# Attention biases loaded in the layer before, a compressed attention branch staged further apart, and more identity products in a two-block transformer kernel

## The chip, the cores and the metric

The kernel runs on one core of a Trainium2 chip. A core has TensorE (PE in the profile, its weight loads PEld), VectorE (DVE), ScalarE (ACT), GpSimd (POOL) and SyncE (SP). Each takes its own instructions in order and waits on semaphores for the others. Data moves from HBM in DMA transfers, which here are issued by ACT and by SP, each on a queue of its own; the profile writes ACTq and SPq for the issuing. The metric is the device time of one execution in microseconds (us). Everything is float32.

## What is computed

Two blocks in a row on 256 tokens of width 1024. The first block has two layers: a sparse attention with three branches (compressed, selected, window; with 256 tokens all four blocks are selected) and a block attention that is plain causal attention at this length. The second block has one layer: eight heads of windowed attention with a table bias and eight heads of 2-D neighbourhood attention with a relative bias, then a retrieval of single-neuron experts (16 384 of them, all evaluated here). The parts that the change touches, cut from the reference:

```
# layer 0, compressed branch
k_cmp = partial_rope(rms_norm(compress(kc, 0), k_g[0]), cos_c, sin_c)
v_cmp = compress(vc, 1)
p_cmp = masked_softmax(einsum('bcgrd,bngd->bcgrn', qc, k_cmp) * scale, m_cmp)
o_cmp = einsum('bcgrn,bngd->bcgrd', p_cmp, v_cmp)
return gc[..., 0:1] * o_cmp + gc[..., 1:2] * o_slc + gc[..., 2:3] * o_win
# every layer
h = rms_norm(x, norm_g[i]) * (1 + scale) + shift        # scale, shift, gate from c @ ada_w
x = x + gate * ((o * silu(z)) @ w_out)
# second block: scores + bias, then softmax; both mixers normalised before w_out
mixed = concatenate([rms_norm(o_a, out_norm_a), rms_norm(o_b, out_norm_b)])
x = x + gate1 * (mixed @ w_out)
```

## The kernel before

Tokens lie in two tiles t of 128. The program is straight-line up to the experts, and one emission order in Python sets the order of instructions on each engine. The stages: layer 0 (sparse attention) to about 245 us of the span, layer 1 to about 375, layer 2 (windowed and neighbourhood attention) to about 515, then the query products and the experts.

**Projections.** A weight tile of 2 MB (`Tile`) is loaded by ACT's queue into one of three ring slots; `load_all` issues the loads of the tiles named in a call. Most tiles are split into a high and a low part (`Parts.step`: ACT copies a quarter to `u_hi` or `v_hi`, DVE forms `u_lo` or `v_lo`), and PE makes three products of them (`project_split`, `project_cols_split`, line 688, 24 products a block of columns). A quarter of the next tile is split while PE works on a block of this one.

**Deferred work.** `soon(work, delay, summed)` puts a piece of work on a list with a due time on `pe_us`, a running estimate of PE's time; `run_later()` emits what is due after each block of products. Work marked `summed` is left out of the `run_later(True, False)` that comes ahead of an attention. In layer 0 the transposes of the queries (L864, copy L866 on ACT) and six stages of the compressed branch are placed so: `run_turns(0)`, `cmp_scores(0)` (L1433: 16 products; its softmax from L1440 to L1463 on DVE with one exponential on ACT), `run_turns(1)`, `cmp_turned(0)` (L1468, copy L1471), `cmp_scores(1)`, `cmp_turned(1)`. They lie among the eight blocks of the z projection, z0 and z1, whose results go through ACT (L1174).

**Adaptive-norm weights.** 80 chunks of 512 KB (`in_ada_t`) come on SP's queue into three buffers; `trickle` emits one DVE step for each (L429), spread over all projections and attentions. When one is used, its buffer's next chunk is asked for.

**Attention.** `attend` walks pairs p of banks: exponentials of p (L965 on DVE, L973 on ACT), the normalising of p-1 (L1001 or L1005), scores of p+1 (L954), outputs of p-2 (L923), transposes of p-1 (L1014, copies L1017 on ACT). At p == 3 it issues the loads of its `loads` argument. `fill_wait(n, b)` (L188) makes n products of the identity with itself into a bank that nobody reads; at p == 1 it is called with fills[0] and fills[1].

**Output stages.** `gated_out.rest` multiplies the attention's result with w_out; near its end, at (t, c) == (1, 5), `turn_next` transposes the next layer's normalised tile 0 (L568), which waits for ACT's scaling (L605). In layer 2 `normed` squares the result (L1627) and `sum_squares` sums it by products with ones (L1640).

**Biases of layer 2.** `bias_a` (1.5 MB) is loaded after the first query products of layer 2, `bias_b` (2 MB) after the second, both on ACT's queue (L156), between the loads of the tiles kb, vb_tile, mix_out0 and mix_out1.

Of the kernel before, what the change touches and what calls it, by code (L numbers as in the profile page):

```python
# [48 lines left out]
LAYER_ROOM = 18027  # L49
TOK = 4  # L50
# [75 lines left out]
def build(nc, st, a, dbg):  # L126
# [28 lines left out]
    def load(dst, src, name, eng=None):  # L155
        return Load(nc, st, name).did((eng or sy).dma_start(dst, src))  # L156
# [47 lines left out]
    def soon(work, delay=0.0, summed=False):  # L204

        item = Pending(work, pe_us[0] + delay, summed)
        later.append(item)
        return item
# [641 lines left out]
    def q_tile_use(qT, j, tab_g, bufs):  # L850

        def use(t, ps, m):
# [4 lines left out]
            def second():  # L857
# [12 lines left out]
                turns[t] = soon(turn_over, TURN_LAG)  # L870
# [218 lines left out]
    def gated_out(first, second, layer, tmp, rstd=None):  # L1089
# [41 lines left out]
        def rest(begin_next, turn_next, place_next, loads):  # L1131
# [8 lines left out]
            for t in range(NT):  # L1140
                x_hi, x_lo = (h[:, :, t * P:(t + 1) * P] for h in (h_hi, h_lo))
                for n, cs in enumerate(halves):
                    b = proj_bank()
                    T.need(b.free, h_split[t])
                    for c in cs:
                        if (t, c) == (NT - 1, DC - 3):
                            turn_next()
                            place_next()
# [67 lines left out]
    with ExitStack() as s0:  # L1216
# [198 lines left out]
        project_split(q1, q_tile_use(qT, 1, row("nsa_q_norm"), qbufs), z0, (z1,))  # L1415
# [70 lines left out]
        def run_stage(n):  # L1486
            f, t = stages[n]
            f(t)
            if n + 1 < len(stages):
                soon(lambda: run_stage(n + 1), (2.5, 3.5, 3.5, 0.5, 7.5)[n])  # L1490

        soon(lambda: run_stage(0), 1.0)
# [30 lines left out]

    with ExitStack() as s1:
# [6 lines left out]
        zT = carve([P, DC, S], s1)  # L1531
        split_h(0, V)
# [13 lines left out]
               causal_bias, lambda h: 3e38, True, [copied["q"], copied["k"]], [copied["v"]], lambda t: None, times_z(zT), tail, (qa,), (1, 3, 1))  # L1546
# [10 lines left out]
    with ExitStack() as s2:  # L1557
        w_in = a["w_in_2"]
        bias_a = carve([P, HA, 3 * P], s2)
        bias_b = carve([P, NT, HB, S], s2)  # L1560
# [15 lines left out]
        m_ba = load(bias_a[:], a["bias_a"], "ld_ba", ac)  # L1576
# [19 lines left out]
        m_bb = load(bias_b[:], a["bias_b"], "ld_bb", ac)  # L1596
# [16 lines left out]
        def bias_of(h, t, w):  # L1613
            return bias_a[:, h, P * (1 - t):P * (3 - t)] if h < HA else bias_b[:, t, h - HA, :]
# [7 lines left out]
        def normed(t, m):  # L1622
# [12 lines left out]
            def sum_squares():  # L1635
                b = spare_bank()
                T.need(b.free, m_s, m_ones)
# [13 lines left out]
        tail, rest = gated_out(mix_out0, mix_out1, 2, [carve([P, 512], s2) for _ in range(NT)], lambda t, half: rstds[:, t, half:half + 1])  # L1651
# [4 lines left out]
               bias_of, lambda h: nsink[:, h:h + 1] if h < HA else 3e38, False, [*m_ready, m_ba, m_bb], [m_vb], lambda t: None,  # L1656
               normed, tail, (query0,), (2, 4, 1), sink=row("sink_a_2"))
# [599 lines left out]
```

## Time and profile before

| | us |
|---|---|
| three runs | 1368.34, 1369.69, 1370.37; median 1369.69 |
| the profiled execution | 1369.69, of it span of the instructions 1368.4 |
| PE busy in the span | 1293.2 (95%) |
| DVE, ACT, POOL busy | 1064.2 (78%), 596.6 (44%), 245.7 (18%) |
| mean granted TensorE clock | 0.985 of full speed |

A row of a timeline gives start and duration in us, engine, line, operation, the tensors and shapes and how many are merged; in brackets stands how long the engine had been idle and who released it. Matmul rows count two for each product in float32. `ACTq` rows are DMA issues: their duration is that of the issuing, not of the transfer. Line numbers are those of the kernel before.

### The profile page before, as it was taken

To read this page: it belongs to the slowest core of one execution; us is meant where nothing else is said; L and a number is where in the kernel's file an instruction comes from. 1 tells how busy PE (TensorE), PEld (TensorE's weight loads), DVE (VectorE), ACT (ScalarE), POOL (GpSimd) and SP (SyncE) were. 2 spreads that over 40 slices of the span, in tenths; PEclk is the share of its full clock that TensorE was granted. 3 is DMA by queue.
4 is the path that set the end of the run, shared out by engine and by line. 5 is a ranking of instruction groups with operands and counts; after the bars stand their busy time and mean duration, and the time that the engine had idled before them with its cause. 6 is when DMAs were issued, how large, how long until landed. Compare 5 with 4: busy or idle time off the path is not lost.

```text
span 1368.4 us, 21907 instructions
## 1 busy us (share of the span) xinstructions
PE 1293.2 (95%) x8261; PEld 1115.5 (82%) x8261; DVE 1064.2 (78%) x2316; ACT 596.6 (44%) x1101; POOL 245.7 (18%) x179
## 2 busy tenths in 40 slices
PE   5888998988998889999999999999999999999997
PEld 5577865685696569999999999999988888888886
DVE  5686796687667788999997888888876667766676
ACT  1534483546343525455544444444343333333332
POOL 0463000360000005689950000000000000000000
PEclk9998899999999989999999999999999999999999
DMA  9867532866379335454444444444465555555552
GB/s 353 307 223 285 190 124 63 290 214 234 128 285 355 108 130 210 156 183 164 173 139 154 141 153 143 151 147 148 154 214 186 185 188 192 189 185 187 189 192 95
DMA packets 92238, 256.82 MB, mean 188 GB/s; under 512 B 9456, under 2 KB 16880, under 8 KB 91760
## 3 DMA queue, kind: packets, MB, share of 16 engines
q1 hardware_dynamic: 59728, 195.91, 41.6%
q10 hardware_dynamic: 32416, 59.66, 12.3%
q8 instruction: 60, 0.98, 0.3%
q14 instruction: 34, 0.28, 0.1%
HBM read 254.47 MB, written 1.06 MB: 187 GB/s over the span
## 4 chain that ended last, share of the span: by engine, by line
PE 61%; DVE 15%; POOL 9%; issue 7%; DMA 5%; ACT 3%; SPq 1%; POOLq 0%; ACTq 0%; DVEq 0%
PE bank L1714 26%; PE bank L1706 19%; PE bank L1986 4%; PE bank L688 3%; PE bank L1118 3%; POOL v_lo L1746 2%; POOL u_lo L1746 2%; DMA arena<-in_w_in 2%; DVE arena L429 2%; DVE arena L965 2%; POOL head_ms L819 2%; DMA arena<-in_nsa_w_in 1%; DVE u_lo L680 1%; PE bank L714 1%; DVE arena L1005 1%
## 5 line engine op out<-in xcount | busy, mean ns | idle before, releaser
L1706 PE MATMUL bank<-h_hi,u_hi 128*128 128x256 f32 x632 | 182.9, 289 | 3.9 <-POOL u_lo L1746 2.9
L1706 PE MATMUL bank<-h_hi,u_lo 128*128 128x256 f32 x632 | 178.9, 283 | 0.0
L1706 PE MATMUL bank<-h_lo,u_hi 128*128 128x256 f32 x632 | 178.8, 283 | 0.0
L1706 PEld LDWEIGHTS bank<-h_hi,u_hi 128*128 128x128 f32 x632 | 121.1, 192 | 4.8 <-POOL u_lo L1746 1.9
L1706 PEld LDWEIGHTS bank<-h_lo,u_hi 128*128 128x128 f32 x632 | 121.2, 192 | 0.0
L1706 PEld LDWEIGHTS bank<-h_hi,u_lo 128*128 128x128 f32 x632 | 121.0, 191 | 0.0
L2169 POOL TENSOR_SCALAR stat<-stat 128x1 f32<-128x1 f32 x2 | 0.4, 190 | 656.8 <-ACT arena L2166 656.8
L2082 ACT ACTIVATE u_hi<-raw 128x1024 fp32r<-128x1024 f32 x64 | 68.1, 1063 | 108.6 <-PE bank L1714 108.6
L2082 ACT ACTIVATE v_hi<-raw 128x1024 fp32r<-128x1024 f32 x64 | 68.0, 1063 | 106.5 <-PE bank L1714 106.5
L1706 PE MATMUL bank<-h_hi,v_hi 128*128 128x256 f32 x392 | 113.0, 288 | 0.9 <-POOL v_lo L1746 0.9
L429 DVE CUSTOM_DVE_ANT_0 arena<-arena 128x1024 f32<-128x1024 f32 x80 | 102.5, 1293 | 11.9 <-DMA arena<-in_ada_t 10.8
L1706 PE MATMUL bank<-h_hi,v_lo 128*128 128x256 f32 x392 | 111.0, 283 | 0.0
L1706 PE MATMUL bank<-h_lo,v_hi 128*128 128x256 f32 x392 | 110.9, 283 | 0.0
L2088 DVE TENSOR_TENSOR v_lo<-raw,v_hi 128x1024 fp32r<-128x1024 f32 x64 | 78.5, 1226 | 25.4 <-ACT v_hi L2082 25.4
L2088 DVE TENSOR_TENSOR u_lo<-raw,u_hi 128x1024 fp32r<-128x1024 f32 x64 | 78.5, 1226 | 25.3 <-ACT u_hi L2082 25.3
L2016 ACT ACTIVATE gate_row<-bank 128x256 f32<-128x256 f32 (+40 forms) x83 | 23.5, 283 | 167.4 <-PE bank L1706 167.4
L1714 PE MATMUL bank<-u_hi,a_hi 128*128 128x512 f32 x256 | 80.7, 396 | 0.6 <-DVE a_lo L1732 0.6
L1714 PE MATMUL bank<-v_lo,a_hi 128*128 128x512 f32 x256 | 80.8, 397 | 0.0
L1714 PE MATMUL bank<-u_lo,a_hi 128*128 128x512 f32 x256 | 80.7, 397 | 0.0
L1714 PE MATMUL bank<-v_hi,a_hi 128*128 128x512 f32 x256 | 80.6, 396 | 0.0
L1714 PE MATMUL bank<-u_hi,a_lo 128*128 128x512 f32 x256 | 80.0, 393 | 0.0
L1714 PE MATMUL bank<-v_hi,a_lo 128*128 128x512 f32 x256 | 80.0, 393 | 0.0
(273 smaller groups left out, 3480.7 us busy)
## 6 DMA issues: line engine op xcount, KB each, us to landing
raw<-in_u SPq DMA_DIRECT2D x128, 512.0 KB, 3.5
raw<-in_v SPq DMA_DIRECT2D x128, 512.0 KB, 4.3
arena<-in_ada_t SPq DMA_DIRECT2D x80, 512.0 KB, 5.5
arena<-in_ada_w SPq DMA_DIRECT2D x12, 512.0 KB, 12.2
raw<-in_nsa_w_in ACTq DMA_DIRECT2D x3, 2048.0 KB, 11.8
arena<-in_moba_w_in ACTq DMA_DIRECT2D x3, 2048.0 KB, 14.4
arena<-in_w_in ACTq DMA_DIRECT2D x3, 2048.0 KB, 10.5
arena<-in_w_query ACTq DMA_DIRECT2D x3, 2048.0 KB, 10.4
```

The costliest lines, as they stand in the source:

```text
L429: m = V.did(ve.tensor_tensor_reduce(out=chunk_buf[i], in0=chunk_buf[i], in1=silu_row, scale=1.0, scalar=0.0, op0=ALU.mult, op1=ALU.add, ac ...
L688: inst = pe.matmul(dst, x, y, start=first and n == 0, stop=last and n == len(pairs) - 1)
L819: return G.did(po.tensor_tensor(hn[0:np_, 0:n], hn[0:np_, 0:n], pow_half[0:np_, 0:n], ALU.pow))
L965: m = V.did(ve.tensor_tensor_reduce(out=probs[k][:, j * w:(j + 1) * w], in0=b.t[:, j * w:(j + 1) * w], in1=bias_of(h, t, w), scale=-1.0, s ...
L1118: last = pe.matmul(b.t[:], hT[:, c, t * P:(t + 1) * P], first.w[:, c, :], start=c == halves[n][0], stop=c == halves[n][-1])
L1706: last = pe.matmul(zbank[k].t[:, 0:S], u[:, c, :], h[:, c, :], start=n == 0, stop=n == 3 * DC - 1)
L1714: last = pe.matmul(outb[2 * t + h].t[:], x[k][:, t * P:(t + 1) * P], quad[slot][y][:, h * 512:(h + 1) * 512], start=b == 0 and n == 0, sto ...
L1746: po.tensor_tensor(quad[slot][1], raw_all[:, slot, :], quad[slot][0].bitcast(F32), ALU.subtract).then_inc(s_ulo, 1)
L1986: last = pe.matmul(gate_bank(g).t[:, j * P:(j + 1) * P], one_hot[:, g % 2, j, :].bitcast(F32), weighted[:, g % 2, j, :], start=True, stop= ...
L2016: last = ac.activation(zpast[k][:, 0:done], zbank[k].t[:, 0:done], ACT.Gelu_apprx_tanh)
L2082: ac.activation(quad[slot][0], raw_all[:, slot, :], ACT.Copy).then_inc(s_vhi, 1)
L2088: ve.tensor_tensor(quad[slot][1], raw_all[:, slot, :], quad[slot][0].bitcast(F32), ALU.subtract).then_inc(s_vlo, 1)
```

## The change

Three things are done. The biases of layer 2 get a fixed place in the arena's last 6400 columns and, for two heads, in `hkT`, and are loaded as three transfers at p == 3 of layer 1's attention, behind the tile qa; the two loads in layer 2 go. In layer 0 the transposes of the second half of the queries are due 30 instead of 10.5 after their block, the six stages get other delays, and the last one may move into the attention. Identity products are added: two at the end of the output stages of layers 0 and 1, four in that of layer 2, one more at p == 1 of layer 2's attention, and one ahead of each of its two sums of squares.

```diff
@@ constants
 LAYER_ROOM = 18027
+BIAS_AT = ARENA - 6400
@@ q_tile_use: the transposes of a block of queries wait for their time
-    def q_tile_use(qT, j, tab_g, bufs):
+    def q_tile_use(qT, j, tab_g, bufs, lag=TURN_LAG):
...
-                turns[t] = soon(turn_over, TURN_LAG)
+                turns[t] = soon(turn_over, lag)
@@ gated_out, rest()
                         if (t, c) == (NT - 1, DC - 3):
+                            fill_wait((2, 2, 4)[layer], banks[4])
                             turn_next()
                             place_next()
@@ layer 0, the calls
-        project_split(q1, q_tile_use(qT, 1, row("nsa_q_norm"), qbufs), z0, (z1,))
+        project_split(q1, q_tile_use(qT, 1, row("nsa_q_norm"), qbufs, 30.0), z0, (z1,))
@@ layer 0, the stages of the compressed branch
             if n + 1 < len(stages):
-                soon(lambda: run_stage(n + 1), (2.5, 3.5, 3.5, 0.5, 7.5)[n])
-
-        soon(lambda: run_stage(0), 1.0)
+                soon(lambda: run_stage(n + 1), (2.5, 2.5, 2.5, 2.5, 14.0)[n], n + 2 == len(stages))
+
+        soon(lambda: run_stage(0), 2.5)
@@ between layer 0 and layer 1
+    bias_a_most = arena[:, BIAS_AT:BIAS_AT + 6 * 3 * P].rearrange("p (h k) -> p h k", h=6)
+    bias_a_rest = hkT[:].rearrange("p i n -> p (i n)").rearrange("p (h k) -> p h k", h=HA - 6)
+    bias_b = arena[:, BIAS_AT + 6 * 3 * P:ARENA].rearrange("p (t h k) -> p t h k", t=NT, h=HB)
+
+    class Biases:
+
+
+        def load(self, e):
+
+            e.need(halves_done, T.last())
+            self.marks = [load(bias_a_most, a["bias_a"][:, 0:6, :], "ld_ba_most", e.eng),
+                          load(bias_a_rest, a["bias_a"][:, 6:HA, :], "ld_ba_rest", e.eng),
+                          load(bias_b, a["bias_b"], "ld_bb", e.eng)]
+
+    biases, halves_done = Biases(), T.last()
@@ layer 1, the loads of its attend
-               causal_bias, lambda h: 3e38, True, [copied["q"], copied["k"]], [copied["v"]], lambda t: None, times_z(zT), tail, (qa,), (1, 3, 1))
+               causal_bias, lambda h: 3e38, True, [copied["q"], copied["k"]], [copied["v"]], lambda t: None, times_z(zT), tail, (qa, biases), (1, 3, 1))
@@ layer 2
-        bias_a = carve([P, HA, 3 * P], s2)
-        bias_b = carve([P, NT, HB, S], s2)
...
         project_cols_by_tile(qa, q_use(0), qb, (kb,), 4)
-        m_ba = load(bias_a[:], a["bias_a"], "ld_ba", ac)
...
         project_cols_split(qb, q_use(HA // 2), kb, (vb_tile, mix_out0))
-        m_bb = load(bias_b[:], a["bias_b"], "ld_bb", ac)
...
         def bias_of(h, t, w):
-            return bias_a[:, h, P * (1 - t):P * (3 - t)] if h < HA else bias_b[:, t, h - HA, :]
+            if h >= HA:
+                return bias_b[:, t, h - HA, :]
+            return (bias_a_most[:, h] if h < 6 else bias_a_rest[:, h - 6])[:, P * (1 - t):P * (3 - t)]
...
             def sum_squares():
                 b = spare_bank()
+                fill_wait(1, b)
                 T.need(b.free, m_s, m_ones)
...
-               bias_of, lambda h: nsink[:, h:h + 1] if h < HA else 3e38, False, [*m_ready, m_ba, m_bb], [m_vb], lambda t: None,
-               normed, tail, (query0,), (2, 4, 1), sink=row("sink_a_2"))
+               bias_of, lambda h: nsink[:, h:h + 1] if h < HA else 3e38, False, [*m_ready, *biases.marks], [m_vb], lambda t: None,
+               normed, tail, (query0,), (2, 5, 1), sink=row("sink_a_2"))
```

PE in layer 0, from the products of the second compression on. `bank<-hkT` are the folds of the hidden layer (L1327) and of the gates (L1392), `128x32 x16` a `cmp_scores`, `ident,arena 128x128 x4` a set of four transposes (L864 queries, L1468 `cmp_turned`); each "..." stands for blocks of 24 products of L688. Before:

```order
L1302 MATMUL bank<-arena 64x256 x24
L864 MATMUL bank<-ident,arena 128x128 x4
L1327 MATMUL bank<-hkT 128x64 x2
...
L1392 MATMUL bank<-hkT 128x48 x2
...
L864 MATMUL bank<-ident,arena 128x128 x4
L1433 MATMUL bank<-arena 128x32 x16
...
L1468 MATMUL bank<-ident,arena 128x128 x4
L954 MATMUL bank<-arena 128x128 x16
```

The same place now (the lines of after.py are one or two further down):

```order
L1304 MATMUL bank<-arena 64x256 x24
L1329 MATMUL bank<-hkT 128x64 x2
...
L1394 MATMUL bank<-hkT 128x48 x2
L865 MATMUL bank<-ident,arena 128x128 x4
...
L1435 MATMUL bank<-arena 128x32 x16
...
L955 MATMUL bank<-arena 128x128 x16
...
L1470 MATMUL bank<-ident,arena 128x128 x4
L924 MATMUL bank<-arena 64x256 x12
```

The first query transposes now come after the gates' fold, one block of z products stands between them and the scores, the second ones a block later still, and the last transposes of the compressed branch have left the place ahead of the attention's scores for one ahead of its first outputs. On the other side of this, the DVE rows at the end of the z projection, from the second softmax's last step on. `ISA arena,ada` is one adaptive-norm chunk (L429). Before:

```order
L1463 TENSOR_TENSOR arena<-arena 128x512
L429 ISA arena,ada<-arena 128x1024
L429 ISA ada 128x1
...
L436 TENSOR_TENSOR ada<-ada,cols 128x4
L1471 COPY arena<-bank 128x512
L965 ISA arena,nmax<-bank,causal 128x128
```

Now, where "..." stands for two more pairs of the same two rows and, before, for one:

```order
L1465 TENSOR_TENSOR arena<-arena 128x512
L430 ISA arena,ada<-arena 128x1024
L430 ISA ada 128x1
...
L437 TENSOR_TENSOR ada<-ada,cols 128x4
L966 ISA arena,nmax<-bank,causal 128x128
```

Four chunks instead of two stand between the second softmax and the attention, and the copy (L1471) is gone from there. ACT in layer 1's attention, p == 3, now:

```order
L281 DMA arena<-in_w_in 128x8x512
L157 DMA arena<-in_bias_a 128x2304
L157 DMA hkT<-in_bias_a 128x768
L157 DMA arena<-in_bias_b 128x4096
L974 ACTIVATE arena,rsum<-arena,nmax 128x256 x4
```

and ACT in layer 2's projections before, from which the two L156 rows are now gone and nothing else:

```order
L280 DMA arena<-in_w_in 128x8x512
L156 DMA arena<-in_bias_a 128x3072
L677 ACTIVATE u_hi<-arena 128x1024
L1571 ACTIVATE arena<-bank 128x256
L280 DMA arena<-in_w_in 128x8x512
L280 DMA raw<-in_w_out 128x8x512
...
L156 DMA arena<-in_bias_b 128x4096
L677 ACTIVATE u_hi<-arena 128x1024 x2
```

Three issues now stand between one pair's copies and the next pair's exponentials in layer 1; in layer 2 the load of vb_tile (second `in_w_in`) has no bias ahead of it.

## Rows read from the trace of the kernel before

**Rows 1.** The page: shares of the chain that ended last, by engine.

```profile
PE 61%; DVE 15%; POOL 9%; issue 7%; DMA 5%; ACT 3%; SPq 1%; POOLq 0%; ACTq 0%; DVEq 0%
```

**Rows 2.** Windows: us, busy PE PEld DVE ACT POOL, PEclk, DMA share, GB/s.

```profile
134.00:144.00 10.00, 10.00 (x77) 9.94 (x78) 6.03 (x15) 4.52 (x6) 0.00 (x0) 0.70 0.48 184
159.00:172.00 13.00, 11.05 (x76) 9.32 (x78) 11.25 (x61) 9.62 (x37) 0.00 (x0) 0.74 0.67 243
502.00:512.00 10.00, 7.36 (x37) 6.03 (x36) 9.54 (x20) 2.65 (x5) 0.56 (x1) 0.83 0.70 258
```

**Rows 3.** Timeline of PE, layer 0, 121 to 165 us.

```profile
122.61 0.66 PE L1327 MATMUL bank<-hkT 128*128 128x64 f32 x4 [0.68 <-DVE arena L1361]
...
133.85 3.62 PE L1433 MATMUL bank<-arena 64*128 64x32 f32 x32 [3.17 <-ACT arena L866]
...
153.56 1.97 PE L1433 MATMUL bank<-arena 64*128 64x32 f32 x32
...
160.95 1.11 PE L1468 MATMUL bank<-ident,arena 128*128 128x128 f32 x4 [2.34 <-DVE arena L1463]
```

**Rows 4.** Timeline of ACT, layer 0, 130 to 134 us.

```profile
130.31 0.27 ACT L1400 ACTIVATE arena<-arena 128x48 f32<-128x48 f32 x1 [0.28 <-DVE arena L1398]
...
133.12 0.59 ACT L866 ACTIVATE arena<-bank 128x512 f32<-128x512 f32 x1
```

**Rows 5.** Timeline of DVE, end of layer 0's z projection and attention's start.

```profile
155.58 0.76 DVE L1440 TENSOR_TENSOR arena<-bank,cmp_mask 128x256 f32<-128x256 f32 x2 [2.95 <-PE bank L1433]
...
160.20 0.69 DVE L1463 TENSOR_TENSOR arena<-arena 128x512 f32<-128x512 f32 x1
...
163.30 0.68 DVE L1471 COPY arena<-bank 128x512 f32<-128x512 f32 x1
164.12 0.29 DVE L965 CUSTOM_DVE_ANT_0 arena<-bank,causal 128x128 f32<-128x128 f32 x1
```

**Rows 6.** Timeline of DVE, start of layer 1's attention.

```profile
314.90 0.29 DVE L965 CUSTOM_DVE_ANT_0 arena<-bank,causal 128x128 f32<-128x128 f32 x1 [1.87 <-PE bank L954]
```

**Rows 7.** Timeline of PE, layer 2, first and last of four such rows.

```profile
418.85 0.50 PE L688 MATMUL bank<-u_hi,h_hi 128*128 128x512 f32 x1 [1.18 <-DVE arena L1600]
...
426.55 0.50 PE L688 MATMUL bank<-v_hi,h_hi 128*128 128x512 f32 x1 [0.95 <-DVE v_lo L680]
```

**Rows 8.** Timeline of ACT and its queue, layer 2, 395 to 420 us.

```profile
398.22 0.38 ACTq L280 DMA_DIRECT2D arena<-in_w_in  x1
...
406.19 6.24 ACTq L156 DMA_DIRECT2D arena<-in_bias_b  x1
...
416.14 2.01 ACT L677 ACTIVATE u_hi<-arena 128x1024 fp32r<-128x1024 f32 x2 [8.63 <-DMA arena<-in_w_in]
```

**Rows 9.** DMA issues of 385 to 440 us: KB each, median us to landing.

```profile
arena<-in_bias_a ACTq DMA_DIRECT2D x1, 1536.0 KB, 15.5
arena<-in_ada_t SPq DMA_DIRECT2D x15, 512.0 KB, 7.2
```

**Rows 10.** DMA issues of 300 to 330 us.

```profile
arena<-in_ada_t SPq DMA_DIRECT2D x8, 512.0 KB, 4.2
arena<-in_w_in ACTq DMA_DIRECT2D x1, 2048.0 KB, 9.0
```

**Rows 11.** Timeline of ACT, layer 1's attention, behind the load at p == 3.

```profile
331.20 0.51 ACT L973 ACTIVATE arena<-arena,nmax 128x256 f32<-128x256 f32 x1 [1.50 <-DVE nmax L965]
```

**Rows 12.** Timeline of DVE, 387 to 430 us, first and last of four such rows.

```profile
395.94 1.23 DVE L429 CUSTOM_DVE_ANT_0 arena<-arena 128x1024 f32<-128x1024 f32 x1 [1.47 <-DMA arena<-in_ada_t]
...
429.41 1.23 DVE L429 CUSTOM_DVE_ANT_0 arena<-arena 128x1024 f32<-128x1024 f32 x1 [2.58 <-DMA arena<-in_ada_t]
```

**Rows 13.** Timeline of PE, layer 2's attention and output stage.

```profile
438.36 2.00 PE L188 MATMUL bank<-ident 128*128 128x256 f32 x8
...
480.67 2.97 PE L1640 MATMUL bank<-ones,arena 128*128 128x1 f32 x16 [1.18 <-ACT arena L1627]
...
505.46 1.97 PE L568 MATMUL bank<-ident,arena 128*128 128x128 f32 x8 [2.60 <-ACT arena L605]
```

More of the change, by code:

```diff
@@ L1531, in build @@
         zT = carve([P, DC, S], s1)
+        assert top[0] <= BIAS_AT, top[0]
         split_h(0, V)
@@ L1649, in normed @@
             return oz_mark[t]
-        tail, rest = gated_out(mix_out0, mix_out1, 2, [carve([P, 512], s2) for _ in range(NT)], lambda t, half: rstds[:, t, half:half + 1])
+        mix_tmp = [carve([P, 512], s2) for _ in range(NT)]
+        assert top[0] <= BIAS_AT, top[0]
+        tail, rest = gated_out(mix_out0, mix_out1, 2, mix_tmp, lambda t, half: rstds[:, t, half:half + 1])
         attend([(lambda h, w: kaT[half_of(h), h // (HA // KVA), 0:w] if h < HA else kbT[half_of(h), (h - HA) // 2, 0:w],
```

## The prediction

> **What bounds the kernel now.** The table of busy times comes first: PE works 1293.2 of 1368.4 us, so what it does not work is 75 us in all, and an edit can only take from that, from products run at the lower clock, or from DVE where DVE sets the pace. The chain that ended last says the same: 61% on PE, 15% on DVE [rows 1]. So I went through the windows for the granted clock and then through PE's timeline for its waits. The reader is to see three places. In layer 0, among the z products, PE waits 0.68, 3.17 and 2.34 us [rows 3], and the clock is at 0.70 and 0.74 of full speed around the last two [rows 2]. In layer 2, from 417 to 427 us, PE waits four times for the split of vb_tile; the first and the last are in [rows 7], and with 0.82 and 0.96 between them they make 3.91 us. At layer 2's end PE waits 2.60 us for ACT's scaling, and the transposes behind it take 1.97 us [rows 13] in a stretch at clock 0.83 [rows 2]. Behind each place PE or DVE goes on without slack, so I let a gain there pass to the end unless a later wait takes it back.
>
> All sums are against the profiled execution, 1369.69 us, which is also the median of the three runs.
>
> **Layer 0, the z projection.** The first wait (0.68) is the fold's for a bank that DVE's copy L1361 empties late; with the query transposes gone from ahead of it, the fold takes the next bank in turn, which is free, and I expect the wait to go. Before, the copy L866 that lets `cmp_scores(0)` go ran at 133.12 for 0.59 us, though ACT had been free of the gates' sigmoid at 130.31 + 0.27 = 130.58 [rows 4]; other ACT work stood between. Now L866 follows the sigmoid directly, ends near 130.58 + 0.59 = 131.2, and `cmp_scores(0)` can start near 131.3 instead of 133.85: 2.55 us sooner, the 0.68 included. The second query transposes stood ahead of that point and now stand behind it; a set of four took 1.11 us in a slow stretch [rows 3], by the ratio of 3.62 to 1.97 some 0.6 at full clock, which is given back: 1.95 remain. `cmp_turned(0)` needs the first softmax. Its work on DVE and ACT ends 5.3 us after it starts (155.58 to 160.89 for the second one [rows 5]), and DVE will start it late by one split of 1.2 us and a rest, I take 1.9 behind the end of the scores. PE in the meantime has two blocks of products where it had four; a block is some 2.9 us (158.61 less the end of the second scores at 155.53 is 3.1, a pipeline's tail in it) [rows 3]. So PE arrives after 2 x 2.9 + 0.6 = 6.4 and the softmax after 7.2 us: a new wait of 0.8. The waits give 1.95 - 0.8, about 1.2 us.
>
> The clock is the unknown. At 0.70 over 134 to 144 us [rows 2] the products lost 0.30 x 10 = 3.0 us; the scores took 3.62 us there and 1.97 at full speed [rows 3]. If a wait of about 1.95 instead of 3.17 us keeps the clock up, all 3.0 come back; if not, none. The trace has no row that decides between them, so I take the middle, 1.5. The z projection, which ended at 160.95 - 2.34 = 158.61, then ends at T = 155.9: 2.7 us sooner, with bounds of 1.2 and 4.2.
>
> **Layer 0, the entry to the attention.** Before, DVE's first L965 came at 164.12, 5.5 us behind the end of the z products: a wait of 2.34 for the softmax, 1.11 of transposes, the copy of 0.68 and the products of scores. Now three blocks instead of one stand behind the second scores, and the softmax, which ends 5.4 us behind its scores, is through at T - 8.7 + 5.4 = T - 3.3. Four chunk steps of 1.23 us [rows 12] then stand on DVE ahead of L965. Three of them end at T + 0.4. The fourth needs the buffer that the first frees at T - 2.1; a chunk lands in 4.2 us [rows 10], so it runs from T + 2.1 to T + 3.3, and L965 follows. That is 2.2 us better than 5.5. Bounds: in layer 1, where no tail of this kind stands, DVE waited for the scores alone [rows 6], and by the scores alone L965 could come at T + 1.8 (3.7 better); with a landing of 7.2 us [rows 9] it comes at T + 6.3 (0.8 worse). Against this stand the transposes and the copy of the last stage, which are now inside an attention in which DVE sets the pace: 0.68 for the copy [rows 5], up to 1.3 if PE's transposes count too. **Layer 0 in sum: 2.7 + 2.2 - 0.7 = 4.2 us.**
>
> **Layer 1.** Three loads are issued on ACT at p == 3. The first load of a bias needs its columns free, which the program ties to the end of layer 0; that is long past. The issue of vb_tile took 0.38 us and that of a bias behind two big loads 6.24 us [rows 8]. Here only qa is ahead, so I take 0.4 to 0.6 each, 1.8 for the three, near the quick row. What is queued behind them is ACT's exponentials of the next pair, which come after an idle time of 1.50 us [rows 11]. So 0.3 us shows. On the other side, 3 x 6.24 = 18.7 us less 1.50 is the price of issues that block; that is a rival below. The 3.5 MB run beside the ada_t chunks. Eight chunks were asked for in 30 us [rows 10], one in 3.75 us, and three buffers lie ahead, so a chunk has some 11 us to land; 4.2 or even 7.2 [rows 9, 10] is within that. I cost it at nothing; what it costs when the cover is gone is a rival too. The two identity products at the output stages of layers 0 and 1 are 0.5 us each: four took 2.00 [rows 13]. They lie in waits for ACT like the one at 505.46; I cost them at nothing, at most 0.5 each.
>
> **Layer 2, the tile vb_tile.** It was issued at 398.22 and landed at 416.14 [rows 8], 17.9 us later. bias_a, 1.5 MB asked for shortly before on the same queue, itself took 15.5 us [rows 9]. A tile of the same 2 MB with no bias beside it landed in 9.0 [rows 10]. Without the bias I expect 9 to 13 us, thus 407 to 411. What it must beat: the split of the last quarter came 3.9 us too late in all, so a landing 3.9 to 4.4 us earlier, before about 411.7, takes all four waits. Both ends are inside; **3.9 us** go, at worst 2 if the transfers of mix_out0 and the chunks hold it back. DVE's waits for chunks in this stretch (1.47, 1.85, 1.11, 2.58; first and last in [rows 12]) get shorter too, but PE does not wait for them, and I count nothing. ACT no longer issues for 0.6 and 6.24 us; it was idle behind that, for 8.63 us [rows 8].
>
> **Layer 2, attention and output.** One more product at p == 1 fits into PE's wait there: nothing, at most 0.5. The product ahead of each sum of squares: the second lies in a wait of 1.18 us [rows 13], the first where DVE sets the pace. Nothing from the waits. The four ahead of the transposes take 4 x 0.5 = 2.0 us of a wait of 2.60, so they delay nothing. If the clock stays up over them, the stretch of 502 to 512 us gets back 0.17 x 10 = **1.7 us** [rows 2]; if not, 0. I take 1.7, because a quarter of the wait or less is left idle.
>
> **The sum.** -4.2 + 0.3 - 3.9 - 1.7 = -9.5: 1360.2 us.
>
> **Rivals.** (1) The restaging only moves its waits: the clock still falls after 1.95 us, and the buffer of the fourth chunk comes late by the 7.2 us row, so that 1.2, the -0.8 and the -0.7 of the copy leave nothing. For it: the wait moved before too, with each stage hanging on ACT and DVE in turn. Then 1360.2 + 4.2 = 1364.4. (2) vb_tile is still late, since mix_out0 is issued right behind it and shares the transfers: +3.9, 1364.1. Against it: it lands behind everything else in its queue only if later loads overtake it. (3) The clock stays up in more places: the other 1.5 of layer 0, and in the second sum of squares, which took 2.97 us [rows 13]; by the ratio of 3.62 to 1.97 [rows 3] it would take 1.6, 1.4 less. 1360.2 - 2.9 = 1357.3. (4) The chunks of ada_t starve in layer 1's attention. In 387 to 430 us, with a bias and two tiles in flight, DVE waited four times for a chunk, 7.0 us in all [rows 12]. The same mix is now moved to where DVE sets the pace: +7.0, 1367.2. Against it stands the 11 us of lead. (5) The slower one: ACT is held in the three issues at p == 3. If each takes the 6.24 us of [rows 8] instead of 0.6, the exponentials of the next pair, and with them DVE and PE, stand for 18.7 - 1.5 = 17.2 us, and the time is 1360.2 - 0.3 + 17.2 = 1377.1. It ends above the time before once the issues hold ACT for more than 9.8 + 1.5 = 11.3 us in all. For it: three big loads stood behind each other in that row, as they do here with qa and two biases. Against it: there the queue had vb_tile and mix_out0, 4 MB, ahead of it; here the third issue has 3.9 MB less one bias, 3.5 MB, ahead, which have been running for a few us.
>
> The Trainium skill bears on rival 4: "DMA: Bandwidth & Descriptors", section "Queues, rings and completion order", says that each transfer engine takes turns between the queues that have work for it, a packet at a time. By that rule the biases on ACT's queue halve what a chunk on SP's queue gets, whatever order they were asked for in; the landing of 7.2 instead of 4.2 us [rows 9, 10] agrees with it, and it does not by itself exceed the lead.
>
> **How the numbers follow.** Forecast 0.38 (1360.2), rival 1 0.20, rival 2 0.10, rival 3 0.17, rival 4 0.08, rival 5 0.07. A measurement of this kernel can tell about 0.2%, 2.7 us, from no change, so faster means below 1367.0. All of the forecast but a hundredth, rival 3, nine tenths of rivals 1 and 2 and about a third of rival 4 lie there: 0.84. The rest of 1, 2 and 4 is within 0.2%: 0.09. Rival 5 is slower: 0.07. The low end takes the best bounds, 7.2 in layer 0 (4.2 + 3.7 - 0.7), 3.9, 1.7 and 1.4, near 1355; the high end takes in rivals 1, 2 and 4, 1367.5. Left out are rival 5 and the tails of the others, some 0.15.
>
> **What would show it.** Right: `cmp_scores(0)` within 2 us behind its block and at 1.97 us; the first L965 of layer 0 near 159; the four waits for the split of vb_tile gone; L568 in layer 2 near 1.1 us; three issues below 0.7 us each at p == 3. Wrong: a new wait of PE for the softmax above 2 us, DVE waiting for ada_t ahead of the attention or inside layer 1's, ACT's first exponential behind the issues more than 1 us late. The prediction fails most easily on the clock, which carries 3.2 of the 9.5 us, and on the length of the three issues.

## The result and the profile after

The changed kernel takes 1360.97 us (median of four runs, 1359.59 to 1362.87) against 1369.68: the ratio is 0.9941, 95% interval 0.9930 to 0.9953, so 8.1 us less. A second measurement gave 0.9938 (0.9925 to 0.9952). The forecast was 1360.2, range 1355 to 1367.5. The profiled execution has a span of 1360.4 us where the one before had 1368.4. Lines of the changed kernel are one or two higher than before (L965 is L966, L1433 is L1435).

The first fence is PE's timeline in layer 0, which answers [rows 3]. The columns are those of the rows before.

```profile
122.52 0.66 PE L1329 MATMUL bank<-hkT 128*128 128x64 f32 x4
...
132.15 1.98 PE L1435 MATMUL bank<-arena 64*128 64x32 f32 x32 [1.19 <-ACT arena L867]
...
141.28 0.66 PE L1470 MATMUL bank<-ident,arena 128*128 128x128 f32 x4 [0.79 <-DVE arena L1465]
...
155.46 2.06 PE L955 MATMUL bank<-arena 64*128 64x128 f32 x32
```

The wait ahead of the fold is gone, the one ahead of the first scores fell from 3.17 to 1.19 us, the scores took 1.98 instead of 3.62, and the new wait for the softmax is 0.79. A wait of 0.45 us at 127.84, for DVE's scaling of the query heads (L827), is new too. PE goes from the z products straight into the attention's scores. The windows answer [rows 2]; the column behind POOL is the granted clock.

```profile
134.00:144.00 10.00, 9.21 (x79) 8.97 (x78) 8.29 (x16) 7.62 (x11) 0.00 (x0) 1.00 0.66 241
159.00:172.00 13.00, 10.75 (x93) 7.49 (x91) 12.09 (x78) 11.58 (x54) 0.00 (x0) 1.00 0.72 268
502.00:512.00 10.00, 9.49 (x85) 9.52 (x86) 5.97 (x12) 5.16 (x8) 0.56 (x1) 1.00 1.04 394
```

All three stretches run at full clock in this trace. In the second trace of the same kernel the first of them has 0.89. DVE's timeline at the entry to the attention, for [rows 5]:

```profile
152.25 0.69 DVE L1465 TENSOR_TENSOR arena<-arena 128x512 f32<-128x512 f32 x1
...
157.59 1.23 DVE L430 CUSTOM_DVE_ANT_0 arena<-arena 128x1024 f32<-128x1024 f32 x1 [1.21 <-DMA arena<-in_ada_t]
...
158.94 0.28 DVE L966 CUSTOM_DVE_ANT_0 arena<-bank,causal 128x128 f32<-128x128 f32 x1
```

The softmax's last step runs before the z products end, and the fourth chunk step waits 1.21 us for its transfer, just ahead of the attention. ACT and its queue in layer 1's attention, and then in layer 2, for [rows 8, 11]:

```profile
325.38 0.60 ACTq L157 DMA_DIRECT2D arena<-in_bias_a  x1
326.01 0.45 ACTq L157 DMA_DIRECT2D hkT<-in_bias_a  x1
326.49 0.51 ACTq L157 DMA_DIRECT2D arena<-in_bias_b  x1
327.11 0.51 ACT L974 ACTIVATE arena<-arena,nmax 128x256 f32<-128x256 f32 x1 [1.50 <-DVE nmax L966]
...
393.75 0.38 ACTq L281 DMA_DIRECT2D arena<-in_w_in  x1
394.30 0.46 ACTq L281 DMA_DIRECT2D raw<-in_w_out  x1
...
408.80 2.01 ACT L678 ACTIVATE u_hi<-arena 128x1024 fp32r<-128x1024 f32 x2 [5.43 <-DMA arena<-in_w_in]
```

The three issues take 1.56 us and end at 327.00, and ACT's exponentials start at 327.11 behind the same 1.50 us of idle time as before. vb_tile needs 15.05 us instead of 17.9. On PE, for [rows 7, 13], one of four waits for its split is left, the second sum of squares (L1658) takes 1.95 us where it took 2.97, and the output stage of layer 2 has lost most of its wait for ACT, but got one for DVE:

```profile
419.21 0.50 PE L689 MATMUL bank<-v_hi,h_hi 128*128 128x512 f32 x1 [0.95 <-DVE v_lo L681]
...
474.47 1.95 PE L1658 MATMUL bank<-ones,arena 128*128 128x1 f32 x16 [0.56 <-ACT arena L1644]
...
495.09 1.89 PE L189 MATMUL bank<-ident 128*128 128x256 f32 x8
497.81 1.10 PE L569 MATMUL bank<-ident,arena 128*128 128x128 f32 x8 [0.84 <-ACT arena L606]
...
502.51 0.68 PE L797 MATMUL bank<-arena 128*128 128x128 f32 x4 [1.53 <-DVE arena L589]
```

Where the time went is read from the starts of the same rows in both traces. The table gives the start in the kernel before and, for others, the difference to it in us; the kernels behind the first two are those of the experiments below, "again" is the changed kernel in its second measurement. The first row stands ahead of everything that any of these kernels changes.

| row | before | changed | again | restage_only | biases_only | fills_only | fill_scores |
|---|---|---|---|---|---|---|---|
| first L1302, layer 0 | 115.94 | +1.25 | -0.37 | +0.42 | +0.43 | +1.00 | -0.51 |
| second scores, layer 0 | 153.56 | -8.83 | -9.59 | -9.10 | +0.59 | +1.26 | -1.75 |
| first L965, layer 0 | 164.12 | -5.18 | -6.53 | -5.92 | +0.37 | +1.26 | -1.98 |
| end of its last L965 | 206.73 | -5.68 | -7.02 | -6.43 | -0.76 | +0.13 | -3.11 |
| first L965, layer 1 | 314.90 | -4.08 | -6.20 | -5.37 | -1.38 | -0.56 | -3.75 |
| end of last L965, layer 1 | 334.70 | -4.08 | -6.21 | -5.37 | -1.38 | -0.57 | -3.75 |
| L568 of tile 1, end of layer 1 | 376.61 | -4.15 | -7.67 | -6.82 | -0.48 | +0.24 | -3.82 |
| first L965, layer 2 | 435.44 | -7.34 | -10.82 | -6.79 | -3.47 | -0.12 | -3.48 |
| end of L568 of tile 0, layer 2 | 507.43 | -8.52 | -13.72 | -7.22 | -2.74 | -2.28 | -3.81 |
| L568 of tile 1, layer 2 | 514.98 | -7.93 | -13.12 | -6.67 | -2.38 | -1.65 | -3.82 |

So: up to the first row, where all seven kernels are the same program, the traces already lie -0.5 to +1.25 us apart from the one before. That is chance, and the changed kernel's trace has the worst of it. Counted from that row, layer 0 gave 6.9 us (1.25 + 5.68; 6.7 in the second trace), 1.5 of it was gone at the end of layer 1, layer 1's attention changed by nothing, the stretch with vb_tile gave 3.2, and layer 2's attention and output gave 1.2 and took 0.6 back. Behind 515 us the difference stays: 7.9 there, 8.0 in the spans.

The trace of the kernel before has bad luck of its own in layer 0's attention. From the first L965 to the end of the last it takes 42.61 us there, with a clock of 0.74 from 159 to 172 us, and 41.48 in biases_only, fills_only and fill_scores, in which this attention is the same as before. In all ten traces with the restaging it takes 42.10 to 42.12 us.

### The profile page after: what moved, and what is told of

Same layout as the page of the kernel before. It is cut to its first block, busy times and chain, and to the rows that moved or that the text cites. A ratio compares the mean times of both kernels' runs of the same rounds, so it can differ in the third digit from the quotient of the medians.

```text
span 1360.4 us, 21954 instructions
## 1 busy us (share of the span) xinstructions
PE 1291.5 (95%) x8283; PEld 1113.5 (82%) x8283; DVE 1063.5 (78%) x2316; ACT 596.0 (44%) x1101; POOL 246.1 (18%) x179
## 4 chain that ended last, share of the span: by engine, by line
PE 61%; DVE 16%; POOL 7%; issue 6%; DMA 5%; ACT 3%; SPq 1%; POOLq 0%; ACTq 0%; DVEq 0%
PE bank L1734 26%; PE bank L1726 21%; PE bank L2006 4%; PE bank L1119 3%; DVE arena L430 2%; PE bank L689 2%; POOL u_lo L1766 2%; DMA arena<-in_w_in 2%; DVE arena L966 2%; POOL head_ms L820 2%; POOL v_lo L1766 2%; DVE u_lo L681 2%; DMA arena<-in_nsa_w_in 1%; DVE v_lo L681 1%; DVE arena L1006 1%
## 6 DMA issues: line engine op xcount, KB each, us to landing
arena<-in_moba_w_in ACTq DMA_DIRECT2D x3, 2048.0 KB, 14.4
arena<-in_w_query ACTq DMA_DIRECT2D x3, 2048.0 KB, 10.5
```

## The experiments

Twelve runs were made, two of them repeats, each against the kernel before on the same chip. The chip was not the same for all. Kernels from different measurements are therefore compared by their ratios to the kernel before. A first group takes the change apart.

**The biases alone**: the kernel before with the class `Biases` and its loads, the other parts undone.

```diff
-        m_ba = load(bias_a[:], a["bias_a"], "ld_ba", ac)
...
-        m_bb = load(bias_b[:], a["bias_b"], "ld_bb", ac)
...
-               causal_bias, lambda h: 3e38, True, [copied["q"], copied["k"]], [copied["v"]], lambda t: None, times_z(zT), tail, (qa,), (1, 3, 1))
+               causal_bias, lambda h: 3e38, True, [copied["q"], copied["k"]], [copied["v"]], lambda t: None, times_z(zT), tail, (qa, biases), (1, 3, 1))
```

> The kernel before with the biases loaded in layer 1's attention and nothing else. Theory A (each part acts alone, the terms add): the four waits for the split of vb_tile shrink by 3.2 us as in the trace of the changed kernel, so 1369.7 - 3.2 = 1366.5, ratio 0.9977; vb_tile lands about 15 us after its issue, three issues at p == 3 take 0.6 or less each and no wait shows behind them. Theory B (vb_tile lands sooner in the changed kernel only because the earlier layers shifted against the chunks): less than 1.5 us, ratio above 0.9989.

Measured: 0.9979 (0.9970 to 0.9988), 2.9 us. The table shows the step from -0.48 to -3.47 between the end of layer 1 and layer 2's attention, 3.0 us, and in the kernels without this part (restage_only, fills_only, fill_scores) a step of -0.4 to +0.3. Theory A holds: this term does not need the other parts.

**The restaging alone.**

```diff
+        project_split(q1, q_tile_use(qT, 1, row("nsa_q_norm"), qbufs, 30.0), z0, (z1,))
+                soon(lambda: run_stage(n + 1), (2.5, 2.5, 2.5, 2.5, 14.0)[n], n + 2 == len(stages))
+        soon(lambda: run_stage(0), 2.5)
```

> The kernel before with only the compressed branch restaged. Theory A: 5.2 to 5.7 us gained up to the end of layer 0's attention, between 0 and 1.6 of them lost in the output stage and in layer 1's projections, so 1364 to 1366, ratio 0.996 to 0.9972. Theory B (a gain in layer 0 is given back further on, since DVE and the chunks set the pace behind it): under 2 us in the end, ratio above 0.9985.

Measured: 0.9955 (0.9941 to 0.9969), 6.2 us. Theory B falls: nearly all that layer 0 gives (6.4 at the end of its attention in the table) arrives. It is a little more than theory A's 0.996 to 0.9972. The trace counted from the first row of the table agrees among all ten runs with this part: the first L965 of layer 0 comes 6.1 to 6.5 us sooner and the end of the last 6.6 to 7.0. What the query transposes bring and what the six stages bring was not tested apart.

**The added identity products alone.**

```diff
+                            fill_wait((2, 2, 4)[layer], banks[4])
+                fill_wait(1, b)
-               normed, tail, (query0,), (2, 4, 1), sink=row("sink_a_2"))
+               normed, tail, (query0,), (2, 5, 1), sink=row("sink_a_2"))
```

> The kernel before with only the added identity products. Theory A: the transposes in layer 2's output stage take 1.1 instead of 1.97 us and the stretch of 502 to 512 us runs at full clock, but DVE's chunk steps stand ahead of the scaling that PE needs next, so PE waits there instead; 0.3 to 1 us in the end, ratio 0.9993 to 0.9998. Theory B (my prediction's term): 1.7 us, ratio 0.9988. Rival: none gained, the added products cost 0.5 us at p == 1 of the attention, ratio 1.0003.

Measured: 0.9989 (0.9980 to 0.9997), 1.5 us, near the 1.7 of the prediction; theory A's lower figure is too low, though the wait it named is there: from -2.28 at the end of the transposes to -1.65 at the next. About 1.0 us of it comes from a place that the prediction costed at nothing, the second sum of squares, which takes 1.95 us as in the changed kernel.

**The changed kernel without them** (the diff above undone in it), run twice, the second time beside the changed kernel itself.

> The changed kernel without its added identity products. Theory A: 0.3 to 1 us slower than the changed kernel, so 1361.3 to 1362, ratio 0.9938 to 0.9944 to the kernel before; L569 in layer 2 takes 1.9 us again. Theory B: 1.7 us slower, 1362.7. If the sum of the first three kernels' gains differs by over 1.5 us from the changed kernel's 8.7, the parts don't simply add.

> The changed kernel without its added products once more. Theory A (the added products are worth 1.5 us alone, as on the kernel before, and nothing in this kernel, since each profile's clock falls at other places): the same as the changed kernel within 1 us, 1360 to 1361.5. Theory B (they add up): 1.5 us slower than it, 1362.5. Theory C (they harm here): 1.5 us faster, 1359.5.

> The changed kernel once more, on the same chip as its variant without the added products. 1361, ratio 0.994. DVE's wait of 0.94 us for a chunk at 235 us stood in one profile of ten; if it is chance it is absent here.

Measured: 0.9926 (0.9913 to 0.9939) and 0.9936 (0.9921 to 0.9951); the changed kernel beside the second 0.9938 (0.9925 to 0.9952). The medians were 1360.55 against 1360.97 and 1361.47 against 1359.75, once one way and once the other. By these times, what the added products are worth in the changed kernel stays open within 2 us. The traces speak for a gain there too: from the first L965 of layer 2 to L568 of tile 1 the eight traces with added products are 0.6 to 2.3 us shorter than the one before, and the five others without them run from 0.3 us shorter to 1.1 longer. The three parts alone sum to 10.6 us, the whole gave 8.1 and 8.5, and with intervals of 1.2 to 1.9 us a part that difference is not clear either. The wait of 0.94 us for a chunk at 235 us was absent in the second profile, as in all the others: chance.

**How much of the restaging is clock?** Five identity products in the kernel before, put into the wait ahead of the first scores, and nothing moved.

```diff
         def cmp_scores(t):
+            if t == 0:
+                fill_wait(5, banks[4])
```

> The kernel before with five identity products put into the wait of 3.17 us ahead of the first scores of the compressed branch, nothing moved. Theory A (a good part of what the restaging gains is clock: 3.62 us of scores against 1.97, and half-speed products behind them): the scores take 2.0 us, the clock of 134 to 144 us is 1.00, cmp1 comes 2.5 to 3 us sooner, so 1366.7 to 1367.2, ratio 0.998. Theory B (the clock costs nothing on the path, DVE's softmax sets it): under 0.5 us.

Measured: 0.9977 (0.9967 to 0.9986), 3.2 us. PE's timeline in this kernel:

```profile
130.08 2.32 PE L188 MATMUL bank<-ident 128*128 128x256 f32 x10
133.40 1.98 PE L1435 MATMUL bank<-arena 64*128 64x32 f32 x32 [1.00 <-ACT arena L866]
```

The scores start at 133.40 (133.85 before; 0.51 us of that was there before the first row of the table) and take 1.98 instead of 3.62 us. The clock of 134 to 144 us rose only to 0.83, not to the 1.00 expected. The first L965 came 1.98 us sooner, 1.5 of it counted from the table's first row. The further 1.1 us within the attention is no effect of the edit: biases_only and fills_only have the same step. So the times say 3.2 us, with an interval of 1.9 to 4.5, and the trace shows 1.5 in the place itself, where the restaging shows 6.1 to 6.5. Theory B is out, since its limit was 0.5. A quarter to a half of what the restaging brings can be had without moving anything.

**What takes 1.6 us back ahead of layer 1's attention?** In the changed kernel's trace 0.8 went at 235 us, where a chunk step of DVE waited 0.94 for its transfer, and PE 1.01 behind it. The other 0.8 is clock. This is PE's wait for GpSimd ahead of a set of query transposes, from the timeline of the changed kernel and then of mixout_late (below), with the attention's first scores, and behind them the window of 290 to 305 us of the one and of the other:

```profile
295.42 0.63 PE L865 MATMUL bank<-ident,arena 128*128 128x128 f32 x4 [2.06 <-POOL arena L839]
...
309.62 2.06 PE L955 MATMUL bank<-arena 64*128 64x128 f32 x32 [0.56 <-ACT arena L1176]
```

```profile
294.43 0.63 PE L865 MATMUL bank<-ident,arena 128*128 128x128 f32 x4 [2.06 <-POOL arena L839]
...
307.14 2.06 PE L955 MATMUL bank<-arena 64*128 64x128 f32 x32 [0.57 <-ACT arena L1176]
```

```profile
290.00:305.00 15.00, 12.94 (x96) 12.76 (x96) 13.44 (x20) 4.03 (x7) 5.19 (x4) 0.89 0.58 183
```

```profile
290.00:305.00 15.00, 12.95 (x109) 12.77 (x109) 12.62 (x21) 3.96 (x8) 4.21 (x4) 1.00 0.66 207
```

The same wait of 2.06 us, once with a clock of 0.89 and once with 1.00. Of the twelve profiles that have this wait (2.04 to 2.07 us), six show 0.89 and six 1.00; the kernel before is among the latter. The price is the same each time: from these transposes to the attention's first scores it is 14.2 us in the six with 0.89 and 12.7 in the other six, 1.5 us. In the trace before 0.66 us had been lost between 247 and 271 us instead, so 0.8 is left as the difference. Part of the gain was so given back by a fall of the clock that the kernel before was spared in its profile.

**Take the wait away**: the second half of the queries of layer 1 turned a block later.

```diff
-        project_split(moba_q1, q_tile_use(qT, 1, row("moba_q_norm"), qbufs), moba_z0, (moba_out0,))
+        project_split(moba_q1, q_tile_use(qT, 1, row("moba_q_norm"), qbufs, 13.5), moba_z0, (moba_out0,))
```

> The changed kernel with the transposes of the second half of the queries in layer 1 due 13.5 instead of 10.5 behind their block, one block of products later. Theory A (the clock falls behind a wait, and the wait of 2.06 us for GpSimd at 293.35 us costs its own length and the 1.15 us that the products behind it ran longer at half clock): both go, about 3 us, so 1358, ratio to the kernel before 0.9915 to 0.993, and the clock of 295 to 305 us is 1.00 again. Theory B (the fall comes from something else than that wait): only the 2 us go and the clock stays at 0.83 there. Theory C (DVE's splits set the pace of these blocks): the time moves into the waits for u_lo and u_hi behind, under 1 us in all.

Measured: 0.9917 (0.9901 to 0.9933), 1358.16 us. Against the changed kernel's 0.9941 this is 3.3 us less, and 2.8 less by the medians; the two intervals still overlap a little. The window of this kernel:

```profile
290.00:305.00 15.00, 14.43 (x124) 14.26 (x124) 12.98 (x20) 4.39 (x10) 4.03 (x3) 1.00 0.67 211
```

PE is busy 14.4 of 15 us where it was 12.9. Theory A's size is met. By the traces 2.2 us of it are sure: mixout_late, with the wait and a full clock, takes that much longer between the two attentions. The other 1.5 is the clock, which stayed at 1.00 in both traces without the wait (this and all_three). As it did so in six of twelve with the wait as well, theory B is not excluded.

**Who holds PE behind the transposes of layer 2?** The two to three chunk steps that `trickle(5)` gives to DVE in each output stage were moved behind the second norm.

```diff
                     load_all(loads)
-                    trickle(5)
...
         finish()
+        trickle(5)
```

> The changed kernel with the adaptive-norm chunk steps of each output stage moved behind the second norm's DVE work, so that DVE scales the first columns (L589) as soon as they are transposed. Theory A (the gain of the added products in layer 2 is given back because three chunk steps stand ahead of L589): PE's waits of 1.53 us at 502.51 and 1.01 at 237.61 go, DVE's chunks then run 0.6 us over its own idle time of 2.8 in front of L656, net 0.5 to 2 us faster, 1359 to 1360.5. Theory B (PE waits there for something else): no gain, or slower by 0.6 a layer, 1362.8.

Measured: 0.9925 (0.9910 to 0.9940), 1358.98 us, 2.0 less than the changed kernel's first median, which the intervals don't tell from it. In its trace PE goes on behind the transposes without a wait, and waits 1.29 us ahead of the next set instead:

```profile
498.15 4.63 PE L797 MATMUL bank<-arena 128*128 128x128 f32 x40
504.07 1.09 PE L569 MATMUL bank<-ident,arena 128*128 128x128 f32 x8 [1.29 <-ACT arena L606]
```

The wait of 1.53 us has moved to the place of the next, and only 0.3 us is won there. In layers 0 and 1 the same thing costs time, since PE now waits ahead of the transposes of tile 1, where it waited 0.27 and 0.33 us in the changed kernel's second trace:

```profile
241.52 1.09 PE L569 MATMUL bank<-ident,arena 128*128 128x128 f32 x8 [1.41 <-ACT arena L606]
...
371.35 1.09 PE L569 MATMUL bank<-ident,arena 128*128 128x128 f32 x8 [1.24 <-ACT arena L606]
```

That is 0.9 us lost in each of the two stages. On the other side, vb_tile landed in 11.45 us in this trace and no wait for its split is left, and the clock of layer 1 stayed at 1.00. That DVE's chunk steps held PE is shown; that moving them makes the kernel faster is not, and in layers 0 and 1 it seems a loss.

**What delays vb_tile?** The load of mix_out0 one tile later.

```diff
-        project_cols_split(qb, q_use(HA // 2), kb, (vb_tile, mix_out0))
+        project_cols_split(qb, q_use(HA // 2), kb, (vb_tile,))
...
-        project_cols_split(kb, kb_use, vb_tile)
+        project_cols_split(kb, kb_use, vb_tile, (mix_out0,))
```

> The changed kernel with the load of mix_out0 issued one tile later, so that only ada_t chunks share the transfers with vb_tile. Theory A (vb_tile took 15.05 instead of 9 us because mix_out0 and the chunks took turns with it): vb_tile lands in 9 to 11 us, the last wait of 0.95 us for its split goes, 0.9 us faster, 1360. Theory B (the chunks alone slow it): still over 13 us and the same time, 1361.

Measured: 0.9936 (0.9920 to 0.9953), 1360.3 us, not told from the changed kernel. ACT in this kernel:

```profile
390.22 0.38 ACTq L281 DMA_DIRECT2D arena<-in_w_in  x1
403.04 1.06 ACT L678 ACTIVATE u_hi<-arena 128x1024 fp32r<-128x1024 f32 x1 [3.55 <-DMA arena<-in_w_in]
```

vb_tile lands in 12.8 instead of 15.05 us and the last wait for its split is gone; the expected 9 to 11 was not reached. That the late load of mix_out0 brought this does not follow from one trace. In the last kernel below, with the same edit, it took 15.5. And with mix_out0 right behind it and no bias beside it, it took 9.9 us in bias_at_output, 11.45 in chunks_behind and 14.65 to 15.3 in the six others. The amount that SP's queue, with the chunks, moved from the issue to the landing goes along with it:

| | landing, us | SP's queue, MB | ACT's queue, MB |
|---|---|---|---|
| bias_at_output | 9.9 | 1.05 | 2.66 |
| chunks_behind | 11.45 | 1.90 | 2.59 |
| changed | 15.05 | 2.58 | 2.61 |
| mixout_late | 12.8 | 2.47 | 2.10 |
| all_three | 15.5 | 3.02 | 2.10 |

ACT's queue moved vb_tile's own 2.1 MB and, where mix_out0 was behind it, some 0.5 MB of that. So mix_out0 took a share, and the chunks the larger one. How much each costs stays open: the chunks were not varied on purpose, and a load that takes longer also has more chunks beside it.

**Where the biases are issued.** Behind the two tiles of layer 1's output stage.

```diff
-               causal_bias, lambda h: 3e38, True, [copied["q"], copied["k"]], [copied["v"]], lambda t: None, times_z(zT), tail, (qa, biases), (1, 3, 1))
+               causal_bias, lambda h: 3e38, True, [copied["q"], copied["k"]], [copied["v"]], lambda t: None, times_z(zT), tail, (qa,), (1, 3, 1))
...
-        rest(begin, turn_first, place_first, (ka_va, qb))
+        rest(begin, turn_first, place_first, (ka_va, qb, biases))
```

> The changed kernel with the three bias loads issued in layer 1's output stage, behind the two tiles ka_va and qb, instead of at p == 3 of its attention. Theory A (an issue blocks ACT when big loads are already queued, as the 6.24 us at 406.19 in the kernel before): the issues take over 8 us together and hold the scaling L606 or the splits behind it, and the 3.5 MB delay ka_va, qb and kb; slower than the changed kernel by 3 to 10 us, 1364 to 1371. Theory B (place does not matter as long as the biases land before layer 2's attention): the same, 1361.

Measured: 0.9954 (0.9940 to 0.9969), 1364.03 us, 3.1 more than the changed kernel by the medians and 1.8 by the ratios, whose intervals overlap. ACT's queue, and PE behind it:

```profile
364.91 1.27 ACTq L157 DMA_DIRECT2D arena<-in_bias_a  x1
366.21 0.46 ACTq L157 DMA_DIRECT2D hkT<-in_bias_a  x1
366.70 3.13 ACTq L157 DMA_DIRECT2D arena<-in_bias_b  x1
369.88 1.51 ACT L584 ACTIVATE arena<-bank,ada,mod_a 128x128 f32<-128x128 f32 x4 [4.93 <-DVE x_tok L1108]
```

```profile
371.53 7.46 PE L797 MATMUL bank<-arena 128*128 128x128 f32 x40 [3.34 <-ACT arena L584]
```

The issues take 4.86 us instead of 1.56, ACT's scaling comes behind them, and PE waits 3.34 us for it. Theory A's mechanism is there in the trace: L568 of tile 1 comes 5.9 us later against its neighbour of tile 0 than before. Part of it is regained up to layer 2's attention, where vb_tile landed in 9.9 us. The price in the end is below theory A's range or at its low end. Rival 5 of the prediction described what happens at another place, not at the one chosen.

**All three edits that looked faster, together.**

> The changed kernel with the three edits together that each gained alone: query transposes of layer 1 a block later, chunk steps behind the second norm, mix_out0 a tile later. Singly they gave about 2.8, 2.0 and 0.7 us against the changed kernel. If they add: 1355.5, ratio 0.9895; if the waits they remove are partly the same DVE time: 1357, ratio 0.9907.

Measured: 0.9898 (0.9885 to 0.9911), 1355.56 us: 14 us less than the kernel before and, by the ratios, 5.9 less than the changed one (0.9898 against 0.9941; their intervals are clear of each other). The sum had 5.5. It is the fastest kernel of the study, but not for the reasons of the sum alone: two waits for the split of vb_tile, 0.96 and 0.94 us, are there in its trace, and the chunk steps cost their 0.9 us in layers 0 and 1. Of the three edits only the first is well supported.

## The prediction, point by point

- **First scores and new wait.** Predicted start 131.3, new wait 0.8. Measured 132.15 and 0.79. Without the 1.25 us lost ahead of layer 0's change the start is 130.9, as in the second profile (130.89). The reading of what the copy L866 stood behind was right.
- **Clock of the z projection.** The middle of 0 and 3.0 us was taken. The stretch ran at 1.00, all 3.0 back; the z products ended just ahead of 155.46 against T = 155.9. With the 1.25 us lost ahead of them that is a gain of 4.4, not 2.7, and a little beyond the bound of 4.2. In six of the ten profiles with the restaging the same stretch shows 0.83 to 0.89, and layer 0 gains the same within 0.5 us, since the scores take 1.98 us in them too. The lower bound, that none comes back, was met in none of them.
- **Entry to the attention.** Predicted T + 3.3, that is 159.2, with the fourth chunk waiting for its buffer. Measured 158.94, 3.5 us behind the scores' start, with that wait: 1.21 us.
- **Layer 0 in sum** was 4.2; measured 6.9 counted from ahead of the change. The term that was too small is the clock, twice: 3.0 instead of 1.5 in the z projection, and 1.1 in the attention, where the trace before ran 159 to 172 us at 0.74 and which no term held. The -0.7 for the last stage's copy was right: the attention takes 42.11 us against 41.48 in the three traces in which it is as before and ran at a clock of 0.87, 0.63 longer. Against the one trace before it looks like a gain of 0.5.
- **Behind layer 0.** "I let a gain there pass to the end unless a later wait takes it back": 1.6 us went ahead of layer 1's attention in this profile, half of it in a chance wait for a chunk, and 0.8 in the second one, from a clock fall that no term held.
- **Issues at p == 3.** 0.3 us was predicted, 0.0 measured; three issues of 0.60, 0.45 and 0.51 us. (The first of them also waits for the last product that PE was given before it, `T.last()`, which the prediction left out; the rows show no wait from it.) A chunk landed in 7.1 us there, as rival 4's row had it, and DVE waited for none. Here the trace agrees with the Trainium skill's page "DMA: Bandwidth & Descriptors", section "Queues, rings and completion order", that the queues take turns, and the lead covered it.
- **vb_tile.** 3.9 us predicted, 3.2 measured (3.0 alone). The landing of 9 to 13 us was the step that failed: it was 15.05. The chunks stayed beside it, and mix_out0 had a smaller share than rival 2 gave it.
- **Fills.** 1.7 predicted. Alone 1.5; the trace of the changed kernel shows 1.2 less 0.6. Two things were missed. DVE has chunk steps ahead of L589, so PE cannot use all that it gains at the transposes. And the product ahead of the second sum of squares, costed at nothing, brought 1.0 us.
- **Rival 3.** Its mechanism came true although the time did not: the other 1.5 of layer 0 came back, and the second sum of squares took 1.95 instead of 2.97 us (1.6 was expected).
- **In all** 9.5 predicted, 8.1 measured, 7.9 in the trace. The sign and the place of each gain were right, the nearness of the number is in part luck. In the trace layer 0 gave 2.7 more than its term; vb_tile gave 0.7 less, the fills and layer 2's attention 1.1 less, the issues gave the 0.3 that they were priced at, 1.5 went in layer 1, and 1.25 had been lost ahead of the change by chance.

## What to carry to other kernels

Look at where a loaded engine issues its DMAs: the same three loads cost 1.56 us behind one tile of 2 MB and 4.86 behind two of 3 MB together, and what counts is who waits behind them. A wait in front of small products costs its length and, in some executions, the clock behind it; before moving the work, try a few idle products in the wait, which here gave a quarter to a half of the gain. A term that rests on the clock should be kept as a range, and looked up in more than one profile. Compare two traces first at a row ahead of the change: here they were up to 1.25 us apart there, and an untouched attention differed by 1.1.

## What was not expected of the hardware

One and the same wait, 2.04 to 2.07 us long and ending between 293 and 301 us, was followed by the lower clock in six of twelve profiles and not in the other six, at a price of 1.5 us. The changed kernel's own runs spread from 1356.5 to 1365.3 us in one measurement, more than the change's 8.1 us; how much of that is such falls was not shown. The issue of the same 2 MB load took 0.51 us with 3.5 MB asked for ahead of it and 3.13 us with 4.5.
